# 32 tokens of a block leave the up products of a mixture-of-experts stage and are dotted on VectorE

## The chip, the cores and the metric

One core of one Trainium2 chip runs the kernel. The metric is the device time of one execution in microseconds (us). The kernel before took 1585.85, 1574.91 and 1577.71 us in three runs, median 1577.71 us.

## What is computed

A transformer block over 512 tokens of width 1024, all in float32: sliding-window attention and a gated delta rule side by side, an output projection, and then PEER, a layer that picks for each token 8 heads x 16 = 128 of 16384 experts. Only PEER is touched:

```
s_top, i_top = lax.top_k(s, 16)                      # per head and half of the query, of 128 keys
best_s, pos  = lax.top_k(sums of all 16 x 16 pairs, 16)
idx  = i1 * 128 + i2 ;  gate = softmax(best_s)
act  = gelu(einsum('tkd,td->tk', u_tab[idx], x))     # 128 dots of width 1024 for each token
out  = einsum('tk,tkd->td', act * gate, v_tab[idx])
```

## The kernel before

The 512 tokens lie in four blocks of 128. Block 0 is done by **gathering**: for each of its 128 pairs of a token, one indirect DMA on GpSimd's queue fetches a row of u and v for each of 128 tokens (8 KB a token, 1.05 MB), VectorE dots the u half with x and adds the v half, scaled, to a sum (`Gathered`, `dot` and `add`; `pair_steps` deals these 256 steps out by a table of rates). Six such rows are in SBUF.

Blocks 1 to 3 (`TD` = 384 tokens) are done **densely**: the table has 128 tiles of 128 experts, and for each tile TensorE multiplies all tokens by the tile's u ("up", 8 slices of the width x 3 products of high and low parts = 24 matmuls of 384 columns), ScalarE takes the gelu, VectorE multiplies by a gate that is zero where the expert was not chosen, and TensorE multiplies by the tile's v ("down", 18 matmuls of 512 columns into six banks). A float32 tile is split before it is multiplied: ScalarE rounds it to the high part, VectorE or GpSimd subtracts to get the low part.

The work runs in two stages behind the projections:

- **Routing** (`routing`). VectorE does the top-k selection, 13 parts for each block (`Selection.part`). For 48 batches of 8 tokens it writes two one-hot arrays (`one_hot`), ScalarE scales one by the gates (`gated`), and TensorE's **gate products** (16 matmul rows of 128 columns in the profile) make the dense gate matrix, which is stored to DRAM. To fill TensorE, the ups of the first `EARLY` = 80 tiles run here: 27 (`FIRST`) before the batches, one with each batch, 5 (`LAST`) after. Their gelus are stored to DRAM. The low parts of tiles 1 to 26 are made on GpSimd, all others on VectorE. A tile has 2 buffers for its parts and 4 (`NU`) for its raw rows; the up of tile t+2 can start only when up t is done, ScalarE has made its high part, and the low part is there.
- **Experts** (`experts`). 48 tiles with up and down, then 80 with the stored gelu and down alone. VectorE makes both low parts, the gate multiplication and the low part of the result, and runs block 0's steps beside (3.1 a tile in the first part, 1.0 in the second).

Orders are written out by hand, the same in each engine's program. Each DMA queue works in order: SP's has the loads and the gate stores, ScalarE's the gelu stores, GpSimd's the fetches. The one-hots compare with a row of 0..127 (`rt_iota_row`) in SBUF.

## Time and profile before

| | before |
|---|---|
| median of three runs | 1577.71 us |
| the profiled execution's span | 1581.1 us |
| PE, busy in matmuls | 1524.7 us, 96% |
| PEld, weight loads | 1388.1 us, 88% |
| DVE | 1326.5 us, 84% |
| ACT | 720.5 us, 46% |
| POOL | 339.2 us, 21% |
| bytes moved by DMA | 384.12 MB, 243 GB/s over the span |

PE is TensorE, DVE VectorE, ACT ScalarE, POOL GpSimd, SP the engine that only issues DMAs. A matmul's recorded duration overlaps its neighbours', so PE's cost is read from the distance between starts; the same holds to a smaller degree for DVE. Up to 409 us the kernel does the projections and the two mixers; nothing of that is touched. Routing runs from 409 to 851 us, the experts from there to 1577 us.

### The profile page before, as it was taken

What the parts mean: (1) busy time and instruction counts of PE and PEld (TensorE: products, weight loads), DVE (VectorE), ACT (ScalarE), POOL (GpSimd) and SP (SyncE); (2) the same over time, 40 slices, a digit from 0 to 9 for tenths busy, and PEclk for the clock granted to TensorE, in tenths of its full rate; (3) what the DMA queues carried; (4) which work ended last, traced back from release to release, by engine and by line L of the source; (5) the groups of instructions that cost most, each with busy time, mean ns of one, the idle gap of its engine ahead of it and who ended that gap; (6) DMA issues with size and microseconds to landing.
All of it is one profiled execution on the core that took longest, in us unless ns stands there. A gap on an engine that the chain in (4) does not pass through costs nothing. (4 is left out here: it accounts for less than half of the span.)

```text
span 1581.1 us, 24984 instructions
## 1 busy us (share of the span) xinstructions
PE 1524.7 (96%) x9451; PEld 1388.1 (88%) x9451; DVE 1326.5 (84%) x2360; ACT 720.5 (46%) x1442; POOL 339.2 (21%) x301
## 2 busy tenths in 40 slices
PE   7999799999999999999998999999999999999999
PEld 6898688889998999989998999999999888888887
DVE  4638777776799999988974999998989999999996
ACT  4553454141344698788763333333333334333332
POOL 4011620010466100301220222222322211111100
PEclk9999899999999999999999999999999999999999
DMA  5220004031444567878998999999998999999982
GB/s 197 86 81 1 8 29 160 30 111 50 132 165 153 168 196 214 316 241 282 366 366 312 334 360 354 341 352 328 372 339 315 354 407 376 380 363 340 351 290 97
DMA packets 152236, 384.12 MB, mean 243 GB/s; under 512 B 11072, under 2 KB 92096, under 8 KB 135488
## 3 DMA queue, kind: packets, MB, share of 16 engines
q1 hardware_dynamic: 122176, 232.75, 41.9%
q0 software_dynamic: 18432, 134.23, 23.4%
q10 hardware_dynamic: 11520, 15.73, 2.7%
q8 instruction: 65, 1.06, 0.3%
q14 instruction: 43, 0.35, 0.1%
HBM read 337.58 MB, written 45.09 MB: 242 GB/s over the span
## 5 line engine op out<-in xcount | busy, mean ns | idle before, releaser
L1795 POOL DMA_INDIRECT scores<-in_peer_uv,pair_index x86 | 126.2, 1468 | 620.2 <-DVE pair_sum L1819 503.2
L1984 PE MATMUL bank<-x_hi,u_split 128*128 128x384 f32 x640 | 220.3, 344 | 10.6 <-POOL u_split L1919 5.5
L1986 PE MATMUL bank<-x_hi,u_split 128*128 128x384 f32 x640 | 215.8, 337 | 0.0
L1985 PE MATMUL bank<-x_lo,u_split 128*128 128x384 f32 x640 | 215.6, 337 | 0.0
L2273 PE MATMUL bank<-v_hi,act_hi 128*128 128x512 f32 x528 | 206.2, 391 | 1.0 <-DVE v_lo L2336 1.0
L2275 PE MATMUL bank<-v_hi,act_lo 128*128 128x512 f32 x528 | 205.9, 390 | 0.0
L2274 PE MATMUL bank<-v_lo,act_hi 128*128 128x512 f32 x528 | 205.7, 390 | 0.0
L2352 DVE TENSOR_TENSOR act_tile<-gelu_tile,onehots 128x384 f32<-128x384 f32 x128 | 118.2, 923 | 43.8 <-ACT gelu_tile L2321 33.1
L2310 ACT ACTIVATE act_hi<-act_tile 128x384 fp32r<-128x384 f32 x128 | 66.6, 521 | 182.0 <-PE bank L2275 130.9
L1984 PEld LDWEIGHTS bank<-x_hi,u_split 128*128 128x128 f32 x640 | 121.0, 189 | 13.0 <-issue 5.9
L2261 PE MATMUL bank<-x_hi,u_split 128*128 128x384 f32 x384 | 129.1, 336 | 1.4 <-PEq L1929 1.4
L2263 PE MATMUL bank<-x_hi,u_split 128*128 128x384 f32 x384 | 129.0, 336 | 0.0
L2262 PE MATMUL bank<-x_lo,u_split 128*128 128x384 f32 x384 | 128.9, 336 | 0.0
L1985 PEld LDWEIGHTS bank<-x_lo,u_split 128*128 128x128 f32 x640 | 120.9, 189 | 0.0
L1986 PEld LDWEIGHTS bank<-x_hi,u_split 128*128 128x128 f32 x640 | 120.8, 189 | 0.0
L2050 ACT ACTIVATE onehot_gated<-onehot_i,rt_smallT 128x128 f32<-128x128 f32 x384 | 117.2, 395 | 6.3 <-DVE onehot_i L2102 4.2
L2275 PEld LDWEIGHTS bank<-v_hi,act_lo 128*128 128x128 f32 x528 | 99.1, 188 | 21.2
L2273 PEld LDWEIGHTS bank<-v_hi,act_hi 128*128 128x128 f32 x528 | 99.1, 188 | 20.7 <-issue 1.4
L2274 PEld LDWEIGHTS bank<-v_lo,act_hi 128*128 128x128 f32 x528 | 99.1, 188 | 19.4
L1819 DVE SCALAR_TENSOR_TENSOR pair_sum<-scores,pair_c,pair_sum 128x1024 f32<-128x1024 f32 x86 | 110.4, 1284 | 1.5
L2336 DVE TENSOR_TENSOR v_lo<-v_raw,v_hi 128x1024 fp32r<-128x1024 f32 x88 | 107.3, 1219 | 0.4 <-ACT v_hi L2304 0.4
L1802 DVE SCALAR_TENSOR_TENSOR scores<-scores,mix 128x1024 f32<-128x1024 f32 x86 | 104.8, 1219 | 0.0
(325 smaller groups left out, 3625.0 us busy)
## 6 DMA issues: line engine op xcount, KB each, us to landing
v_raw<-in_peer_v SPq DMA_DIRECT2D x128, 512.0 KB
u_raw<-in_peer_u SPq DMA_DIRECT2D x64, 512.0 KB, 7.0
u_raw_more<-in_peer_u SPq DMA_DIRECT2D x64, 512.0 KB, 6.7
gates<-gate_stage SPq DMA_DIRECT2D x24, 1024.0 KB, 6.0
onehots<-gates SPq DMA_DIRECT2D x32, 768.0 KB, 8.9
early_gelus<-early_gelu ACTq DMA_DIRECT2D x80, 192.0 KB
gelu_tile<-early_gelus SPq DMA_DIRECT2D x80, 192.0 KB
w_raw<-in_w_in SPq DMA_DIRECT2D x9, 1024.0 KB, 5.2
```

What stands on the lines that cost most here:

```text
L1795: pool.indirect_dma_start(self.slot(k), None, self.table, bass.IndirectOffsetOnAxis(ap=self.sidx[:, k:k + 1], axis=0)).then_inc(self.lande ...
L1984: nc.tensor.matmul(banks.bank(g)[:, 0:TD], uh[:, q, w], m.xh[:, k, P:], start=(k == 0), stop=False)
L1985: nc.tensor.matmul(banks.bank(g)[:, 0:TD], uh[:, q, w], m.xl[:, k, P:], start=False, stop=False)
L1986: t = nc.tensor.matmul(banks.bank(g)[:, 0:TD], ul[:, q, w], m.xh[:, k, P:], start=False, stop=(k == KD - 1))
L2050: ins = nc.scalar.activation(og[:, slot(b, k), t, :], oi[:, slot(b, k), t, :], ACT.Copy, scale=smallT[:, b % 2, 1, k * BT + t:k * BT + t + 1])
L2261: nc.tensor.matmul(bank, uh[:, q, w], m.xh[:, k, P:], start=(k == 0), stop=False)
L2262: nc.tensor.matmul(bank, uh[:, q, w], m.xl[:, k, P:], start=False, stop=False)
L2263: t = nc.tensor.matmul(bank, ul[:, q, w], m.xh[:, k, P:], start=False, stop=(k == KD - 1))
L2273: nc.tensor.matmul(bank[:], ah[:, s, w], v_hi[:, c], start=first, stop=False)
L2274: nc.tensor.matmul(bank[:], ah[:, s, w], v_lo[:, c], start=False, stop=False)
L2275: t = nc.tensor.matmul(bank[:], al[:, s, w], v_hi[:, c], start=False, stop=last)
L2352: nc.vector.tensor_tensor(af[:], ge[n % NG2][:], gt[:, it % 2, :, jj], ALU.mult).then_inc(gate_f, 1)
```

## The change

- 32 tokens (`NS`) of block 1 are no longer columns of the ups: each of the 128 tiles' 24 up matmuls has 352 columns (`TU`) in place of 384. The downs, the gate products and their one-hots stay as wide as they were.
- For these tokens their 32 x 128 chosen u rows are fetched: 32 indirect DMAs of 128 rows of 4 KB (`UpRows.fetch`), four sets of 32 pairs side by side in the 128 partitions. VectorE dots each with x (`UpRows.dot`), which a product with four unit matrices has laid four times over into two PSUM banks (`m.xs`). To have the indices of the four sets in place, six small DMAs are issued on GpSimd's queue (`move`). The activations times gates, transposed, take the place of the gates of these tokens in their four batches, which come last now, and so their column of the dense gate matrix is the finished activation.
- `EARLY` is 96: 21 ups before the batches, two with each batch whose number is below 32 and not 2 modulo 3, one with the others, 5 after. 54 more low parts in the batches are GpSimd's, tiles 1 to 20 as well: 74 in all.
- Selection goes through the blocks in the order 1, 2, 3, 0. Block 0's rows can be fetched only after that, behind all of GpSimd's low parts.
- The row 0..127, the row starts and the index steps, which VectorE reads together with a tile in SBUF, lie in PSUM bank 7; the routing stage has five banks for its products, not eight.
- The gelu stores go from ScalarE's queue to SP's, each behind the load of a later tile.
- In the experts' stage ScalarE copies each tile's gates into a contiguous tile (`copy_gate`), and VectorE multiplies in place there. There are 32 tiles with ups and 96 without; block 0's steps run at 3.1 and then at 1.5 a tile.

```diff
-EARLY = 80
+EARLY = 96
...
+NS = 32
+NR = P // NS
+TU = TD - NS
+CHOICE = [1, 2, 3, 0]
 GRP4 = 2
...
+    def place_constants(self, dve, bank):
+
+        link = self.link(dve)
+        self.iota, self.row0 = bank[:, 0:NK], bank[:, NK:NK + TOPK]
+        self.step = bank[:, 256:512].rearrange("p (q h a) -> p q h a", q=2, h=PH)
+        link(self.nc.vector.tensor_copy(self.iota, self.iota_made[:]))
+        link(self.nc.vector.tensor_copy(self.row0, self.row0_made[:]))
+
...
+
+        nc, link = self.nc, sel.link(dve)
+        link(nc.vector.scalar_tensor_tensor(sel.column[:], sel.small[:, 0, :], float(NK), sel.small[:, 2, :],
+                                            ALU.mult, ALU.add))
+        link(nc.vector.tensor_scalar(sel.column[:], sel.column[:], 2.0, None, ALU.mult))
+        nc.vector.tensor_copy(self.idx[0:NS, :], sel.column[0:NS, 0:NS])
+        nc.vector.tensor_copy(self.gate[0:NS, :], sel.small[0:NS, 1, 0:NS])
+        nc.vector.tensor_copy(sel.moved[0:NS, NS:], sel.column[0:NS, NS:]).then_inc(self.chosen, 1)
+
+    def move(self, pool, sel):
+
+        pool.wait_ge(self.chosen, 1)
+        for r in range(1, NR):
...
+            pool.dma_start(self.gate[rows, :], sel.small[0:NS, 1, cols]).then_inc(self.moved, 16)
+
+    def wait_moved(self, eng):
+        eng.wait_ge(self.moved, 2 * 16 * (NR - 1))
+
+    def fetch(self, pool, k):
+        n = len(self.slots)
+        if k >= n:
...
+            ap=self.idx[:, k:k + 1], axis=0)).then_inc(self.landed[k % n], 16)
+
+    def dot(self, dve, k):
+        n = len(self.slots)
+        dve.wait_ge(self.landed[k % n], 16 * (k // n + 1))
+        row = self.slots[k % n]
+        self.nc.vector.scalar_tensor_tensor(row, row, 1.0, self.xs, ALU.mult, ALU.mult,
...
-    in_first = todo[:sel.PARTS - AHEAD + sel.PARTS]
-    behind_1 = todo[len(in_first):][:4]
-    left = todo[len(in_first) + len(behind_1):]
+    LATE = 2 * NBT
+    ups_in = [1 if n >= LATE or n % 3 == 2 else 2 for n in range(NB_)]
+    FIRST = EARLY - sum(ups_in) - LAST
+    ups_of = [list(range(FIRST + sum(ups_in[:n]), FIRST + sum(ups_in[:n + 1]))) for n in range(NB_)]
+
+    pool_lows = list(range(1, FIRST)) + [t for n in range(LATE) for t in ups_of[n]]
...
+                def store_gelu(n):
+                    banks.wait_taken(sp, ("up", n))
+                    sp.dma_start(gelus[n], ge[:, n % 2, 0:TU]).then_inc(nxt.ge_out[n % 2], 16)
...
-                pool.wait_ge(sel.scores_read, 1)
+                def pool_low(t):
+                    pool.wait_ge(u_hi, t + 1)
+                    if t == 1:
+                        wait_low(pool, 0)
+                    u_low(nc.gpsimd, t).then_inc(low_by_pool, 1)
+
+                fetched = len(up_rows.slots)
+                for t in range(1, FIRST):
+                    pool_low(t)
+                    if t == TURN_1 + 2:
+                        up_rows.move(pool, sel)
+                    if t == TURN_1 + 3:
+                        up_rows.wait_moved(pool)
+                        for k in range(fetched):
+                            up_rows.fetch(pool, k)
+                for n in range(LATE):
+                    for t in ups_of[n]:
+                        pool_low(t)
+                    for k in range(fetched, min(NS, fetched + DOTS)):
+                        up_rows.fetch(pool, k)
+                        fetched += 1
+                pool.wait_ge(sel.chosen_0, 1)
+                pool.wait_ge(up_rows.dots, NS)
                 for k in range(nxt.fetched):
                     pairs_of_0.fetch(pool, k)
 
@@ -1977,14 +2101,13 @@
...
+                sel.place_constants(dve, ps[7])
...
-                pairs_out(1)
+                up_rows.choose(dve, sel)
+                for b, part in in_2:
+                    if part == 5:
+                        pairs_out(1)
+                    if part == 9:
+                        up_rows.wait_moved(dve)
+                    sel.part(dve, b, part)
+                    if part >= sel.PARTS - DOTS_FIRST:
+                        up_rows.dot(dve, part - sel.PARTS + DOTS_FIRST)
                 first_keys(0)
-                for b, part in behind_1:
-                    sel.part(dve, b, part)
-                dve.wait_ge(u_lo, FIRST)
-                early_low(FIRST)
                 for n in range(NB_):
                     if n + 1 < NB_:
                         first_keys(n + 1)
-                    wait_products(dve, n)
+                    wait_products(dve, n - RING)
                     one_hot(oj, n, 2).then_inc(oj_ready, 1)
-                    early_low(early(n) + 1)
+                    for t in range(ups_of[n][-1] + 1, EARLY - LAST if n + 1 == NB_ else ups_of[n + 1][-1] + 1):
+                        if not low_count[t][0]:
+                            early_low(t)
+                    if n + 1 == NB_:
+                        early_low(EARLY - LAST)
                     if n in beside:
                         sel.part(dve, *beside[n])
                     for c in small_after(n - 1):
                         pairs_out(c)
-                    if n >= 2 * NBT:
-                        pairs_of_0.vector_steps(dve, steps[n - 2 * NBT])
+                    for k in dots_in[n]:
+                        up_rows.dot(dve, k)
+                    if n == COEFS - 1:
+                        up_rows.coefficients(dve)
+                    if n == COEFS + 1:
+                        coefs_out()
+                    if n >= LATE:
+                        pairs_of_0.vector_steps(dve, steps[n - LATE])
                 for n in range(EARLY - LAST + 1, EARLY + 1):
                     early_low(n)
 
...
+                def copy_gate(n):
+                    it, jj = n // BODY, n % BODY
+                    if jj == 0:
+                        act.wait_ge(g_in[it % 2], 32 * (it // 2 + 1))
+                    if n >= 2:
+                        act.wait_ge(gated, n - 1)
+                    else:
+                        act.wait_ge(nxt.ge_out[n], 16 * (EARLY // 2))
+                    nc.scalar.activation(af[n % 2][:], gt[:, it % 2, :, jj], ACT.Copy).then_inc(gate_cols, 1)
...
+                    dve.wait_ge(gate_cols, n + 1)
+                    nc.vector.tensor_tensor(af[n % 2][:, NS:], ge[n % NG2][:], af[n % 2][:, NS:], ALU.mult).then_inc(gate_f, 1)
...
-        rates = [2.0] * (P // 8) + [1.0, 2.0] + [3.1] * (NK - EARLY - 2) + [1.0] * EARLY
+        rates = [2.0] * (P // 8) + [1.0, 2.0] + [3.1] * (NK - EARLY - 2) + [1.5] * EARLY
```

The order of instructions shows this at three places. First GpSimd's program at the start of routing, `u_split` being the low parts. Before:

```order
L1919 TENSOR_TENSOR u_split<-u_raw,u_split 128x1024 x2
L1919 TENSOR_TENSOR u_split<-u_raw_more,u_split 128x1024 x2
L1919 TENSOR_TENSOR u_split<-u_raw,u_split 128x1024 x2
L1919 TENSOR_TENSOR u_split<-u_raw_more,u_split 128x1024
L1795 DMA scores<-in_peer_uv,pair_index 128x2048 x4
L1795 DMA pair_rows<-in_peer_uv,pair_index 128x2048 x2
L1795 DMA scores<-in_peer_uv,pair_index 128x2048 x4
```

After:

```order
L2008 TENSOR_TENSOR u_split<-u_raw,u_split 128x1024
L1868 DMA up_index<-shared_index_moved 32x32
L1869 DMA up_gate<-rt_small 32x32
L1868 DMA up_index<-shared_index_moved 32x32
L1869 DMA up_gate<-rt_small 32x32
L1868 DMA up_index<-shared_index_moved 32x32
L1869 DMA up_gate<-rt_small 32x32
L2008 TENSOR_TENSOR u_split<-u_raw,u_split 128x1024
L1878 DMA pair_rows<-in_peer_uv,up_index 128x1024 x4
L2008 TENSOR_TENSOR u_split<-u_raw_more,u_split 128x1024 x2
```

Six small DMAs and then four fetches now stand between low parts that TensorE waits for. The second place is VectorE's program for two early batches, beside which parts of the selection run. Before:

```order
L1392 MAX top<-scores 128x8 x16
L2102 TENSOR_TENSOR onehot_i<-rt_iota_row,rt_smallT 128x1024
L2102 TENSOR_TENSOR onehot_j<-rt_iota_row,rt_smallT 128x1024
L1919 TENSOR_TENSOR u_split<-u_raw,u_split 128x1024
L1397 MAX_INDEX top_index<-top,scores 128x8 x16
L2102 TENSOR_TENSOR onehot_i<-rt_iota_row,rt_smallT 128x1024
L2102 TENSOR_TENSOR onehot_j<-rt_iota_row,rt_smallT 128x1024
L1919 TENSOR_TENSOR u_split<-u_raw_more,u_split 128x1024
```

After:

```order
L2244 TENSOR_TENSOR onehot_i<-bank,rt_smallT 128x1024
L2244 TENSOR_TENSOR onehot_j<-bank,rt_smallT 128x1024
L1401 MAX top<-scores 128x8 x16
L1885 SCALAR_TENSOR_TENSOR pair_rows,up_s<-pair_rows,banks 128x1024 x2
L2244 TENSOR_TENSOR onehot_i<-bank,rt_smallT 128x1024
L2244 TENSOR_TENSOR onehot_j<-bank,rt_smallT 128x1024
L1406 MAX_INDEX top_index<-top,scores 128x8 x16
L1885 SCALAR_TENSOR_TENSOR pair_rows,up_s<-pair_rows,banks 128x1024 x2
```

The low part is gone, two dots with fetched rows (`pair_rows`) stand in its place, and the one-hots read a bank. The third place is SP's DMA queue between two gate stores. Before:

```order
L1937 DMA u_raw<-in_peer_u 128x1024
L1937 DMA u_raw_more<-in_peer_u 128x1024
L1949 DMA gates<-gate_stage 128x16x128
L1937 DMA u_raw_more<-in_peer_u 128x1024
L1937 DMA u_raw<-in_peer_u 128x1024
L1949 DMA gates<-gate_stage 128x16x128
```

After:

```order
L2042 DMA gates<-gate_stage 128x16x128
L2029 DMA u_raw_more<-in_peer_u 128x1024
L2035 DMA early_gelus<-early_gelu 128x352
L2029 DMA u_raw<-in_peer_u 128x1024
L2035 DMA early_gelus<-early_gelu 128x352
L2029 DMA u_raw<-in_peer_u 128x1024
L2035 DMA early_gelus<-early_gelu 128x352
L2042 DMA gates<-gate_stage 128x16x128
L2029 DMA u_raw_more<-in_peer_u 128x1024
```

A gelu store stands behind every load of a tile now, in the same queue.

## Rows read from the trace of the kernel before

**Rows 1.** Windows; busy us of PE, PEld, DVE, ACT, POOL; clock, DMA share, GB/s.
```profile
532.00:824.00 292.00, 285.61 (x1911) 282.95 (x1911) 273.65 (x569) 235.91 (x586) 37.89 (x20) 1.00 0.81 271
...
851.00:1235.00 384.00, 384.00 (x1963) 351.70 (x1963) 346.71 (x435) 137.91 (x223) 104.53 (x71) 1.00 0.93 339
1235.00:1577.00 342.00, 340.96 (x1492) 279.67 (x1491) 314.05 (x393) 124.25 (x184) 40.19 (x36) 1.00 0.89 330
```
**Rows 2.** Timeline of PE (start, duration in us, engine, line), experts' stage.
```profile
1003.77 0.39 PE L2273 MATMUL bank<-v_hi,act_hi 128*128 128x512 f32 x1
...
1007.86 0.34 PE L2261 MATMUL bank<-x_hi,u_split 128*128 128x384 f32 x1
...
1012.02 0.39 PE L2273 MATMUL bank<-v_hi,act_hi 128*128 128x512 f32 x1
```
**Rows 3.** Timeline of PE in the query product, 256 columns wide.
```profile
384.74 0.28 PE L1551 MATMUL bank<-x_hi,w_oq_h 128*128 128x256 f32 x1
...
388.46 0.28 PE L1552 MATMUL bank<-x_lo,w_oq_h 128*128 128x256 f32 x1
```
**Rows 4.** Timeline of PE, routing; in brackets the idle time before and its releaser.
```profile
408.98 0.45 PE L1984 MATMUL bank<-x_hi,u_split 128*128 128x384 f32 x1 [0.19 <-DVE u_split L1919]
...
532.86 1.95 PE L2011 MATMUL bank<-onehot_j,onehot_gated 128*128 128x128 f32 x16
...
815.87 1.95 PE L2011 MATMUL bank<-onehot_j,onehot_gated 128*128 128x128 f32 x16
...
821.81 1.95 PE L2011 MATMUL bank<-onehot_j,onehot_gated 128*128 128x128 f32 x16
...
835.13 0.41 PE L1984 MATMUL bank<-x_hi,u_split 128*128 128x384 f32 x1 [3.05 <-DVE u_split L1919]
```
**Rows 5.** DVE groups by form (busy us, mean ns), of 409:508 and of 530:715.
```profile
L1443 DVE TENSOR_TENSOR selectors<-selectors,index_steps 128x256 f32<-128x256 f32 x32 | 28.4, 957 | 0.1
...
L1443 DVE TENSOR_TENSOR selectors<-selectors,index_steps 128x256 f32<-128x256 f32 x32 | 11.1, 421 | 0.0
```
**Rows 6.** Timeline of POOL: low parts, then fetches of rows.
```profile
437.19 4.08 POOL L1919 TENSOR_TENSOR u_split<-u_raw_more,u_split 128x1024 fp32r<-128x1024 f32 x1 [1.72 <-ACT u_split L2030]
...
455.32 2.44 POOL L1919 TENSOR_TENSOR u_split<-u_raw_more,u_split 128x1024 fp32r<-128x1024 f32 x1 [1.72 <-ACT u_split L2030]
...
640.27 8.49 POOL L1795 DMA_INDIRECT scores<-in_peer_uv,pair_index  x1 [116.03 <-DVE top_index L1397]
649.06 0.94 POOL L1795 DMA_INDIRECT scores<-in_peer_uv,pair_index  x1 [0.30 <-issue]
...
736.79 1.68 POOL L1795 DMA_INDIRECT scores<-in_peer_uv,pair_index  x1 [80.60 <-DVE pair_sum L1819]
```
**Rows 7.** Windows within those stages, same columns.
```profile
1250.00:1310.00 60.00, 60.00 (x264) 49.22 (x263) 57.18 (x73) 23.53 (x35) 8.10 (x8) 1.00 1.02 401
1310.00:1400.00 90.00, 90.00 (x395) 73.91 (x394) 86.71 (x111) 34.76 (x52) 11.24 (x11) 1.00 0.99 373
1400.00:1500.00 100.00, 100.00 (x439) 82.06 (x438) 93.04 (x116) 36.19 (x55) 14.45 (x12) 1.00 0.97 349
743.00:827.00 84.00, 83.27 (x559) 82.79 (x558) 75.39 (x85) 63.26 (x158) 23.04 (x14) 1.00 1.04 367
```
**Rows 8.** DMA issues, 415:505 and 790:850; last number: median us to landing.
```profile
u_raw_more<-in_peer_u SPq DMA_DIRECT2D x10, 512.0 KB, 3.5
...
u_raw<-in_peer_u SPq DMA_DIRECT2D x5, 512.0 KB, 14.7
```
**Rows 9.** DVE groups by form of 1400:1500, then of 0:409.
```profile
L2352 DVE TENSOR_TENSOR act_tile<-gelu_tile,onehots 128x384 f32<-128x384 f32 x24 | 22.2, 923 | 2.6
...
L2356 DVE TENSOR_TENSOR act_lo<-act_tile,act_hi 128x384 fp32r<-128x384 f32 x24 | 13.4, 559 | 4.2 <-ACT act_hi L2310 4.2
L1819 DVE SCALAR_TENSOR_TENSOR pair_sum<-scores,pair_c,pair_sum 128x1024 f32<-128x1024 f32 x8 | 10.3, 1284 | 0.1
...
L1701 DVE TENSOR_TENSOR acc<-acc,bank 128x512 f32<-128x512 f32 x8 | 5.5, 686 | 5.6 <-PE bank L1553 5.6
```

More of the change, by code:

```diff
@@ L340, in _ @@
                 pool.wait_ge(pads, 1)
-                link = chain(pool, plink, [0])
+                link = chain(pool, *m.own["pool"])
                 for b in range(TB):
@@ L362, in _ @@
             def _(act):
-                link = chain(act, alink, [0])
+                link = chain(act, *m.own["act"])
                 def split_w(n):
@@ L470, in _ @@
             def _(dve):
-                link = chain(dve, vlink, [0])
+                link = chain(dve, *m.own["dve"])
                 def split_w(n):
@@ L955, in _ @@
                         level(l, b)
-                link = chain(pool, plink, [0])
+                link = chain(pool, *m.own["pool"])
                 for b in range(TB):
@@ L964, in _ @@
             def _(dve):
-                link = chain(dve, vlink, [0])
+                link = chain(dve, *m.own["dve"])
                 def att_max(b):
@@ L1186, in _ @@
             def _(dve):
-                link = chain(dve, vlink, [0])
+                link = chain(dve, *m.own["dve"])
                 def z_gain(b):
@@ L1266, in _ @@
             def _(pool):
-                link = chain(pool, plink, [0])
+                link = chain(pool, *m.own["pool"])
                 for b in range(TB):
@@ L1682, in _ @@
                 sel.constants(pool)
-                link = chain(pool, plink, [0])
+                for r in range(NR):
+                    nc.gpsimd.tensor_copy(m.repeat[0:NS, r * NS:(r + 1) * NS], m.ident[0:NS, 0:NS])
+                link = chain(pool, *m.own["pool"])
                 for b in range(TB):
@@ L2084, in _ @@
                             sel.exps(act, b)
-                evict(NB_ - 1)
-                pairs_of_0.scalar_steps(act, steps[NBT - 1])
+                    if n == LAST_DOT + 1:
+                        up_rows.gelu(act)
                 for n in range(EARLY - LAST, EARLY):
@@ L2392, in hybrid_layer @@
         m.mem = mem
+        m.own = {name: (sem(f"{name}_in_order"), [0]) for name in ("dve", "pool", "act")}
         m.ident = mem.take("ident", [P, P])
         m.neg_half = mem.take("neg_half", [P, 1])
+        m.repeat = mem.take("unit_rows", [P, P])
         m.upper = mem.take("upper", [P, P])
```

371 lines of the change are left out of this document (217 added, 154 removed).

## The prediction

> **What bounds the kernel.** I read the windows by stage first. In the experts' stage TensorE is busy in every microsecond (384.00 of 384) and in the routing stage nearly so (285.61 of 292), with VectorE close behind (346.71 and 273.65) [rows 1]. Then the timeline of PE, for the distance between starts. In the experts' stage 18 downs of 512 columns take 4.09 us, 227 ns each, and 24 ups of 384 columns take 4.16 us, 173.3 ns each [rows 2]. The query product of 256 columns starts 31 matmuls in 3.72 us, 120.0 ns each [rows 3]. That is 13.3 ns and 0.417 ns a column over the whole range, so a narrower up is cheaper in full proportion. Last I read where TensorE waits in routing: the first gate products start at 532.86, 123.9 us after the first up, and 28 ups of 4.16 make 116.5 of it, so 7.4 are waits; one undisturbed batch takes 5.94 us, 47 batches last 288.95 us, so 9.8 are waits; one late load costs 3.05 us near the end [rows 4].
>
> **The ups.** 128 tiles x 24 matmuls x 32 columns x 0.417 ns = **-41.0 us**; an up then takes 3.84 us. The number of ups does not change, only 16 of them move ahead of the experts' stage, at the same price. The gate products stay at 5.94 - 4.16 = 1.78 us a batch.
>
> **The start of routing.** 22 ups lie before the first gate product now, 84.5 us. Each up needs its predecessor but one, a high part on ScalarE and a low part on GpSimd (2.44 us [rows 6]). About 1.4 us of GpSimd's time a tile is free (3.84 - 2.44). Between low parts 12 and 13 stand the six small DMAs. The first fetch of the old kernel took 8.49 us, one right behind it 0.94, with 0.30 between them [rows 6], so I take 8.49 + 5 x 1.24 + 0.30 = 15.0 us; less the free 1.4 that is 13.6 late for low part 13, and up 13, gelu 13 and every later split queue behind it. The four fetches behind low part 13 are 5.0, 3.6 late. With 0.1 a tile for the tighter chain (2 us) and 2 us for a clock that may fall in a pause of 13 us, TensorE waits 21 us there, against 7.4: **+14 us**. VectorE's part of this stage hides under it: it has four parts of selection fewer, four dots more, and its products of selectors with index steps ran at 957 ns beside GpSimd's low parts and at 421 ns without them [rows 5]. Bounds: if nothing is paid for the first DMA and VectorE is then what is waited for, +2; if the indirect form pays its own 7.5, +21.
> The Trainium skill (GPSIMD Engine Reference, Instruction dispatch) says that the first call of freshly loaded GpSimd code pays about 6 us more. The row's 8.49 against 0.94 agrees in kind; with the page's 6 the sum would be 1.5 us lower.
>
> **The batches.** VectorE loses the low part of each of the first 32 batches and gets two dots in 14 of them. GpSimd does two low parts and two fetches in a batch with two ups: 4.9 + 2 x 1.24 to 2 x 1.68 [rows 6] = 7.4 to 8.2 us of the batch's 2 x 3.84 + 1.78 = 9.46. A fetch stands behind the second low part of its batch, and the dot in VectorE's same batch waits for its landing; the unloaded landing of a 0.5 MB load is 3.5 us, with full queues 14.7 [rows 8]. Behind the dots VectorE has the next one-hots, for which the gate products wait. From one batch's second up over high part, low part, fetches, landing, dots and one-hots I count about 13 us and the landing, for two batches of 16.2 us in the mean: a landing of 4 us is hidden, 6 us is not. The one-hot reads its constant from a bank; VectorE's sum with a bank takes 686 ns for 512 columns [rows 9], no more a column than two tiles in SBUF, so 0. I take 7 us of waits for the 9.8 of before, **-3 us**; the ends are -6 and, with landings of 7 us in 14 batches, +15.
>
> **The end of routing.** From 743 to 827 the queues moved 367 GB/s at a DMA share of 1.04, with TensorE just fed [rows 7]. The old kernel fetched block 0's first six rows at 640, in slack. The new one can do so only behind the last low part of batch 31. From there to the last up I count 8.4 MB of u, 2.9 of gelus, 8.4 of gates, 2.1 of v, 20 rows of 1.05 MB and 4.3 for the five last ups: 47 MB, of which 4 may land later. 43 MB at 367 GB/s are 117 us; TensorE's work there is 16 x 5.62 + 5 x 3.84 = 109. A part of the wait was there before (3.05 us [rows 4]): **+7 us**, between 0 and 15. Gelu stores sit behind loads in SP's queue now; where these land after 14.7 us [rows 8], the gelu of two tiles later waits for its buffer, which is in the upper end.
>
> **The last tiles.** In the 96 tiles without ups a tile takes TensorE 4.09 us. It needs 0.524 MB of v, 0.197 of gates, 0.180 of gelu and 0.75 rows of 1.049: 1.69 MB, 412 GB/s, for the 85 tiles in which 128 steps of block 0 are left. Before it was 1.44 MB. The most that was moved while TensorE stayed full was 401 GB/s over 60 us [rows 7]: 85 x 1.69 / 401 = 358 us, not 348. **+10 us**; 0 if more can be moved, +37 at the 373 GB/s of the next window [rows 7]. VectorE is a second bound at the same place: 93.04 us in 100 [rows 7] or 3.81 a tile, less 0.41 for the gate multiplication (923 ns from a strided tile, a contiguous one 559 [rows 9]), plus half a step of 1.28 [rows 9]: 4.04 of 4.09.
> The Trainium skill (SBUF — State Buffer, A bandwidth-pool intuition) gives about 358 GB/s from HBM to one core; the tail would cost 52 us more by it. The trace moved 401, so the measurement decides.
>
> **Sum.** -41 + 14 - 3 + 7 + 10 = -13 us against the profiled span of 1581.1, which lies 3.4 over the median. From the median 1577.7 that is 1564.7; I forecast 1564 us, 0.9% faster.
>
> **Rivals.**
> - *Small insertions and transfers are hidden.* The six DMAs cost little, or more than 401 GB/s can be moved. -41 + 2 to 6 - 3 + 3 + 3 gives about 1542 to 1548. For it: TensorE did not wait once in the 60 us at 401 GB/s. Against it: 8.49 us is in the rows.
> - *The last tiles are bound by transfers.* At 373 GB/s the sum is 27 higher, 1591. For it: that window followed the one at 401, and the share was 0.99; against it, less was asked for there.
> - *GpSimd becomes the bound* (slower). A low part took 4.08 us where VectorE's products with two operands in SBUF ran beside it [rows 6, 5]. At 4.1 us a batch with two ups needs 8.2 + 3.0 = 11.2 us of GpSimd for 9.46, 1.7 too much in ten batches and 17 us; at the start the chain is 0.8 a tile longer, 16 us. That gives 1564 + 33 = 1597. It decides from a mean of 3.2 us on. Against it: these operands lie in a bank now, and with them VectorE reads SBUF once. The Trainium skill (SBUF — State Buffer, Who interferes with whom) says the same: only a VectorE instruction with two inputs in SBUF, or in a two-port mode, blocks GpSimd's reads. By that rule low parts stay near 2.44; the trace agrees with its first half.
> - *The change does not do what it says:* if a narrow up keeps its 173.3 ns, because the weights' load sets the pace, all else costs 28 us and it is 1605. Against it: 120.0 ns at 256 columns [rows 3].
>
> **Chances.** The forecast's case 0.5, from 1552 to 1576; hidden 0.2; tail bound by transfers 0.13; GpSimd 0.13; no cheaper up 0.04. About 1% is what a measurement of this kernel can tell from no change: below 1562 is faster, above 1593.5 slower. Faster: 0.2 and not quite half of 0.5, 0.43. Slower: 0.15. Same: 0.42. The range from 1538 to 1592 leaves out GpSimd's case and the last one, and the low edge of the hidden one.
>
> **What would show it.** Up starts 160 ns apart; a pause of some 13 us of TensorE near 455 us with GpSimd in its six DMAs; the first gate product near 512; low parts of 2.4 to 2.6 us; products with index steps near 421 ns throughout; VectorE's dots in the first 14 batches waiting for a row by 1 to 3 us or not at all; loads landing after 12 us and more from 800 us on; tiles of 4.2 us in the last stage at about 400 GB/s, with VectorE over 95% busy. The forecast is wrong if low parts pass 3.2 us, if the tail's tiles are 4.09 us or over 4.4, or if TensorE's pause at the six DMAs isn't there.

## The result and the profile after

The changed kernel took 1586.06 us, the median of seven runs (1583.91 to 1589.55), against 1580.68 us for the kernel before in seven runs beside it. The ratio is 1.004 with a 95% interval of 1.0021 to 1.0059. It is a little slower, where 0.9% faster was forecast. The profiled spans are 1582.4 us after and 1581.1 before.

The page of the changed kernel, its part on engines:

```profile
PE 1502.0 (95%) x9438; PEld 1354.3 (86%) x9438; DVE 1242.8 (79%) x2392; ACT 826.7 (52%) x1571; POOL 462.7 (29%) x391
```

TensorE has 22.7 us less of recorded work than before and is not done sooner. VectorE has 84 us less. So the totals do not say where the time went. The same stretches as in [rows 1], cut where the changed kernel changes its pace (columns as there):

```profile
408.00:502.00 94.00, 89.08 (x535) 86.49 (x535) 91.86 (x380) 39.77 (x58) 60.77 (x33) 0.98 0.60 192
502.00:650.00 148.00, 132.77 (x862) 129.94 (x861) 121.87 (x348) 91.86 (x213) 88.15 (x54) 0.97 0.84 274
650.00:790.00 140.00, 140.00 (x958) 140.00 (x958) 85.28 (x245) 97.64 (x228) 71.81 (x33) 1.00 0.71 217
790.00:890.00 100.00, 91.51 (x624) 89.64 (x623) 88.28 (x100) 71.31 (x185) 13.51 (x15) 0.97 1.05 390
1185.00:1225.00 40.00, 34.24 (x141) 27.45 (x140) 31.77 (x46) 19.78 (x28) 7.41 (x6) 0.91 1.01 409
1225.00:1500.00 275.00, 275.00 (x1196) 223.80 (x1195) 262.82 (x383) 162.38 (x227) 61.93 (x50) 1.00 1.02 413
```

TensorE runs short most in the second, the fourth and the fifth row, and the granted clock falls a little there. In the third and the last it is full, in the last at 413 GB/s. The timeline of PE has the places themselves, the answers to [rows 2] and [rows 4]:

```profile
461.17 0.40 PE L2108 MATMUL bank<-x_hi,u_split 128*128 128x352 f32 x1 [1.45 <-POOL u_split L2008]
468.58 0.40 PE L2108 MATMUL bank<-x_hi,u_split 128*128 128x352 f32 x1 [3.33 <-POOL u_split L2008]
...
501.67 1.05 PE L2127 MATMUL bank<-onehot_j,onehot_gated 128*128 128x128 f32 x8
...
815.76 2.05 PE L2127 MATMUL bank<-onehot_j,onehot_gated 128*128 128x128 f32 x8 [6.46 <-ACT onehot_gated L2183]
...
914.00 0.40 PE L2420 MATMUL bank<-x_hi,u_split 128*128 128x352 f32 x1 [2.26 <-PEq L2021]
...
1003.92 0.33 PE L2420 MATMUL bank<-x_hi,u_split 128*128 128x352 f32 x1
...
1007.76 0.39 PE L2432 MATMUL bank<-v_hi,act_hi 128*128 128x512 f32 x1
...
1011.89 0.33 PE L2420 MATMUL bank<-x_hi,u_split 128*128 128x352 f32 x1
...
1212.12 0.77 PE L2432 MATMUL bank<-v_hi_late,act_hi 128*128 128x512 f32 x1 [5.76 <-DVE v_lo_late L2508]
```

24 ups take 3.84 us (1003.92 to 1007.76), as forecast, and a tile with up and down 7.97 us (1003.92 to 1011.89) for the old 8.25. So I add up TensorE's waits: the length of a stretch, less 3.84 us for each up (4.16 before) and 1.78 for each batch's gate products. For the experts it is 7.93 or 4.09 a tile (8.25 before). A fall of the clock is in the wait.

| TensorE's waits, us | before | after | difference | forecast |
|---|---|---|---|---|
| first up to first gate product | 7.4 | 9.1 | +1.7 | +14 |
| batches up to 780 us | 8.5 | 23.7 | +15.2 | -3 |
| last batches and last five ups | 7.7 | 19.1 | +11.4 | +7 |
| experts | 3.7 | 18.6 | +14.9 | +10 |
| sum | 27.3 | 70.5 | +43.2 | +28 |

Against 43.2 us of new waits stand 41.0 us of narrower ups. The first up also started 0.85 us earlier (408.13 against 408.98). That makes +1.3, and so do the spans. The medians lie 5.4 us apart.

### The profile page after: what moved, and what is told of

It reads as the page before. It is cut to its first block, busy times and chain, and to the rows that moved or that the text cites. A ratio compares the mean times of both kernels' runs of the same rounds, so it can differ in the third digit from the quotient of the medians.

```text
span 1582.4 us, 25236 instructions
## 1 busy us (share of the span) xinstructions
PE 1502.0 (95%) x9438; PEld 1354.3 (86%) x9438; DVE 1242.8 (79%) x2392; ACT 826.7 (52%) x1571; POOL 462.7 (29%) x391
## 4 chain that ended last, share of the span: by engine, by line
PE 59%; DVE 6%; DMA 3%; issue 2%; POOL 1%; SPq 1%; ACT 1%; ACTq 0%; DVEq 0%; POOLq 0%
PE bank L2433 7%; PE bank L2434 7%; PE bank L2432 7%; PE bank L2108 6%; PE bank L2109 6%; PE bank L2110 6%; PE bank L2127 4%; PE banks L2432 3%; PE banks L2433 3%; PE banks L2434 3%; PE bank L2420 2%; PE bank L2422 2%; PE bank L2421 2%; DMA v_raw<-in_peer_v 1%; DVE pair_sum L1828 1%
## 5 line engine op out<-in xcount | busy, mean ns | idle before, releaser
L2108 PE MATMUL bank<-x_hi,u_split 128*128 128x352 f32 x768 | 258.3, 336 | 7.1 <-POOL u_split L2008 4.8
L2109 PE MATMUL bank<-x_lo,u_split 128*128 128x352 f32 x768 | 250.5, 326 | 0.0
L2110 PE MATMUL bank<-x_hi,u_split 128*128 128x352 f32 x768 | 250.0, 326 | 0.0
L2479 ACT ACTIVATE act_tile<-onehots 128x384 f32<-128x384 f32 x128 | 122.3, 955 | 62.3 <-DVE act_lo L2521 58.0
L2008 POOL TENSOR_TENSOR u_split<-u_raw,u_split 128x1024 fp32r<-128x1024 f32 x37 | 89.9, 2430 | 135.3 <-ACT u_split L2165 77.0
L2432 PE MATMUL bank<-v_hi,act_hi 128*128 128x512 f32 x320 | 124.8, 390 | 1.2 <-DVE v_lo L2508 1.2
L2127 PE MATMUL bank<-onehot_j,onehot_gated 128*128 128x128 f32 x768 | 102.8, 283 | 23.7 <-issue 15.2
L2434 PE MATMUL bank<-v_hi,act_lo 128*128 128x512 f32 x320 | 125.3, 392 | 0.0
L2127 PEld LDWEIGHTS bank<-onehot_j,onehot_gated 128*128 128x128 f32 x768 | 97.0, 197 | 28.4 <-issue 28.0
L2008 POOL TENSOR_TENSOR u_split<-u_raw_more,u_split 128x1024 fp32r<-128x1024 f32 x37 | 89.8, 2428 | 73.2 <-ACT u_split L2165 73.1
L2463 ACT ACTIVATE v_hi<-v_raw 128x1024 fp32r<-128x1024 f32 x80 | 84.2, 1053 | 14.4 <-DMA v_raw<-in_peer_v 14.1
## 6 DMA issues: line engine op xcount, KB each, us to landing
v_raw<-in_peer_v SPq DMA_DIRECT2D x128, 512.0 KB, 10.6
```

Source lines behind the costliest of these rows:

```text
L2008: return on.tensor_tensor(ul[:, n % 2, :], u_raw[n % NU], uh[:, n % 2, :].bitcast(F32), ALU.subtract)
L2108: nc.tensor.matmul(out, uh[:, q, w], m.xh[:, k, P + NS:], start=(k == 0), stop=False)
L2109: nc.tensor.matmul(out, uh[:, q, w], m.xl[:, k, P + NS:], start=False, stop=False)
L2110: t = nc.tensor.matmul(out, ul[:, q, w], m.xh[:, k, P + NS:], start=False, stop=(k == KD - 1))
L2127: t = nc.tensor.matmul(banks.bank(g)[:, q * NK:(q + 1) * NK], og[:, n % RING, 4 * i + q, :], oj[:, n % RING, 4 * i + q, :], start=True, st ...
L2432: nc.tensor.matmul(bank[:], ah[:, s, w], v_hi[:, c], start=first, stop=False)
```

## Who waits for whom

Between 501 and 650 us, the waits of the changed kernel (in all, times, longest):

```profile
DVE pair_rows L1885 <- DMA pair_rows<-in_peer_uv,up_index: 25.4, 12, 6.6
ACT onehot_gated L2183 <- DVE onehot_i L2244: 25.1, 12, 4.7
PE bank L2127 <- issue: 15.2, 10, 3.2
```

VectorE waits for a fetched row. ScalarE then waits for VectorE's one-hots. For TensorE's waits the profile names no releaser ("issue"), but its gate products need the one-hots of both. The row of `UpRows.fetch` (all 32 of its fetches) says why, and beside it stands what a load of u took in that stretch:

```profile
DMA to landing us min/median/max: 5.3/6.7/9.1
...
u_raw<-in_peer_u SPq DMA_DIRECT2D x12, 512.0 KB, 4.2
```

A fetch of 0.52 MB by 128 indices landed after 6.7 us in the median (6.9 for the 28 of this stretch), a plain load of as much after 4.2. At the hand-over to block 0, from 790 to 890 us:

```profile
ACT early_gelu L2175 <- DMA early_gelus<-early_gelu: 25.4, 9, 7.6
...
PE bank L2127 <- ACT onehot_gated L2183: 8.3, 4, 6.5
```

ScalarE stands before a gelu whose buffer a store has not left. In the experts' stage, SP's queue, ScalarE and the v loads near the hole at 1212:

```profile
1185.23 0.53 SPq L2392 DMA_DIRECT2D h_rows<-h_spill  x1
...
1188.04 0.33 SPq L2358 DMA_DIRECT2D v_raw<-in_peer_v  x1
...
1209.66 1.06 ACT L2463 ACTIVATE v_hi_late<-v_raw 128x1024 fp32r<-128x1024 f32 x1 [7.48 <-DMA v_raw<-in_peer_v]
```

From 1154 to 1227 us the v loads landed after 8.9 us in the median and after 21.6 at the longest. The longest is the load issued at 1188.04: it lands at 1209.64, where ScalarE goes on. 2.8 us ahead of it stands the residual h, 2.1 MB. The kernel before reads h at the same place of its program (four tiles into its last stage):

```profile
1259.90 0.50 SPq L2233 DMA_DIRECT2D h_rows<-h_spill  x1
```

It paid nothing there: TensorE was full from 1250 to 1310 us [rows 7].

## Experiments

All twelve are edits of the changed kernel. Ratios are against the kernel before, run on the same chip. The changed kernel itself stands at 1.004 (1586.06 us), with an interval of 1.0021 to 1.0059. The runs came in four sets, in which the kernel before took 1576.6 to 1579.6 us in the median. So a time of one set against a time of another is good to some 2 us.

**The dots one batch later.**

```
-        dots_in[(k - DOTS_FIRST) // DOTS].append(k)
-    LAST_DOT = (NS - 1 - DOTS_FIRST) // DOTS
+        dots_in[(k - DOTS_FIRST) // DOTS + 1].append(k)
+    LAST_DOT = (NS - 1 - DOTS_FIRST) // DOTS + 1
```

> The changed kernel with one edit: in the batches each pair of dots with fetched rows is one batch later on VectorE (batches 1 to 14), so that a row has a batch longer to land; the fetches stay. In the changed kernel's trace VectorE stood 25.4 us before 12 of its dots for rows that landed 6.7 us after their issue, and TensorE had 22 us of waits between 501.7 and 648 us. Theory A (landing of the rows): both go, the time is 15 to 22 us lower, near 1567. Theory B (GpSimd's queue of two low parts and two fetches, 7.4 to 8.2 us a batch, is what holds the batches): the dots' waits go, but the gate products wait as before for one-hots behind low and high parts, and the time is within 5 us of the changed kernel's, 1581 to 1587.

1566.54 us, ratio 0.9906 [0.987, 0.9943]. This one edit makes the changed kernel faster than the one before. Waits from 501 to 650 us:

```profile
DVE pair_rows L1885 <- DMA pair_rows<-in_peer_uv,up_index: 6.5, 6, 2.0
```

TensorE's waits between the first gate product and 660 us fell from 23.6 to 6.2 us, though the rows landed no sooner (7.0 us in the median for 6.9). At the hand-over to block 0 they grew by some 4 us. Theory A holds: the landing was what the loop could not hide. Theory B falls, because GpSimd's queue was as full as before.

**The gelu stores on ScalarE's queue.**

```
-                    store_gelu(n)
...
+                    banks.wait_taken(act, ("up", n))
+                    act.dma_start(gelus[n], ge[:, n % 2, 0:TU]).then_inc(nxt.ge_out[n % 2], 16)
```

> The changed kernel with one edit: the gelu stores go from ScalarE's own queue again, as in the kernel before. In the changed kernel's trace ScalarE stood 41.3 us in 17 places before a gelu whose buffer a store in SP's queue still held (7.6 us at 805, where TensorE then waited 6.5), none in the kernel before. Theory A (the store's place behind loads and gate stores in one queue): those waits fall to under 5 us, the hand-over at 795 to 831 us loses its 11 us of TensorE's waits and the last ups 2 to 4 of their 6; the time is 10 to 16 us lower, 1570 to 1576. Theory B (the DMA engines themselves are full there, share 1.04 to 1.06, whichever queue asks): the waits move to loads, tiles or rows, and the time is at most 3 us lower.

1583.18 us, ratio 1.0018 [0.9994, 1.0043]. That is 3 us under the changed kernel, with intervals that overlap. The last ups did lose 4.6 of their 6.1 us of waits. The hand-over kept its 12.8, with another wait in the gelu's place:

```profile
817.10 0.60 ACT L2192 ACTIVATE gate_stage<-bank 128x512 f32<-128x512 f32 x1 [10.24 <-DMA gates<-gate_stage]
```

So Theory B at the hand-over: whichever store is next there comes late. The queue alone was not its cause.

**h read back ten tiles before the end.**

```
-                    if n == NMT + 4:
+                    if n == NK - 10:
```

> The changed kernel with one edit: the residual h (2.1 MB) is read back ten tiles before the end, not four tiles into the last stage, where no rows of block 0 are fetched any more. In the changed kernel's trace one v tile landed 21.6 us after its issue at 1200 us, 15 us behind that transfer, and TensorE stood 5.8 us and then ran at 1.2 GHz for a while: a tile of 10.00 and one of 6.34 us for two of 4.15. Theory A (the 2.1 MB in front of the v loads in a stage that moves 412 GB/s anyway): the hole goes, 7 to 8 us less, 1578 to 1579. Theory B (the last stage asks for more than can be moved until its buffers have run dry once): the hole comes at another place, and the time stays within 2 us of 1586.

The expectation puts the late v load's issue at 1200 us; it was 1188.04. 1579.47 us, ratio 1.000 [0.9983, 1.0017], 6 us less. The window of the hole:

```profile
1185.00:1225.00 40.00, 40.00 (x176) 32.66 (x175) 39.23 (x57) 23.45 (x33) 9.14 (x8) 1.00 1.02 416
```

PE is busy 40.00 of 40 where it was 34.24, and no hole came elsewhere in that stage, whose waits fell from 18.6 to 10.6 us. Theory A.

**All ups 384 columns wide again** (the gelu still takes 352 of them).

```
-    q, out = n % 2, banks.bank(g)[:, 0:TU]
+    q, out = n % 2, banks.bank(g)[:, 0:TD]
```

> The changed kernel with one edit: all ups multiply 384 columns again, and the gelu takes the 352 of them that it took; all else, the fetched rows too, is as changed. It prices the narrowing alone. Prediction's term (0.417 ns a column): the time is 36 to 41 us higher, 1622 to 1627; starts of ups 173 ns apart. Rival (TensorE's waits for rows, stores and low parts are in part filled by wider ups, so that the narrowing is worth less in this kernel than its columns): 20 to 33 us higher, 1606 to 1619, with fewer waits between 501 and 650 us.

1612.47 us, ratio 1.0192 [1.0152, 1.0232]. That is 26 us more (24 by the ratios), not 41: the rival. The 96 ups up to the experts' stage cost 30.7 us more, but TensorE's waits there fell from 51.9 to 40.3. So a third of what the narrow ups save was time in which wide ones would have covered a wait. In the experts' stage the price came to 7.9 us.

**Block 0's first six rows, one a batch from batch 26 on.**

```
+    ROWS_AT = [(26 + k, k) for k in range(6)]
...
+                    for at, k in ROWS_AT:
+                        if at == n:
+                            pairs_of_0.fetch(pool, k)
```

> The changed kernel with one edit: block 0's first six rows (1.05 MB each) are fetched one behind each of GpSimd's low parts of batches 26 to 31, not all behind the last. In the changed kernel they were issued from 779.4 to 786.4 us, and from 785 on the queues moved 386 and 397 GB/s at a share of 0.99 and 1.05; gelu stores, loads of u and gate stores then landed late, and TensorE had 11 us of waits from 795 to 831. Moving the gelu stores alone did not help: the gate store behind which ScalarE waited took 17.9 us then. Theory A (the burst of six rows fills the DMA engines just where 2.1 MB of v are read too): with the rows landing before 780, TensorE's waits there fall to 0 to 3 us, the time to 1575 to 1578. Theory B (the steady demand behind batch 32, a row and a half a batch, u, v, stores, is what the engines can't keep up with): the same wait comes a few batches later, and the time stays within 3 us of 1586.

1581.94 us, ratio 1.0012 [0.999, 1.0035], 4 us less with intervals that overlap, between the two theories. First the window of the hand-over in the changed kernel, then in this one:

```profile
785.00:820.00 35.00, 27.33 (x178) 26.79 (x177) 23.66 (x29) 18.42 (x46) 5.69 (x5) 0.91 1.03 402
```

```profile
785.00:820.00 35.00, 33.64 (x239) 33.48 (x238) 32.56 (x36) 24.57 (x63) 3.75 (x4) 1.00 0.99 347
```

Without the burst TensorE is nearly full there. Of the 13.0 us of waits behind 780 us 7.7 were left, now from 817 to 832 us, and 2.4 had moved ahead of 780.

**The four v tiles spread over batches 37 to 46.**

```
-                        for i in range(len(m.v_raw)):
+                    if n in (LATE + 5, LATE + 8, LATE + 11, LATE + 14):
```

> The changed kernel with one edit: the first four v tiles of the experts' stage (0.52 MB each) are read at batches 37, 40, 43 and 46, not all four at batch 32. Theory A (these four loads, in front of the gelu store in SP's queue, are what TensorE waits for by 6.5 us at 815.8): the hand-over loses 5 to 8 of its 11 us of waits, the time is 1578 to 1581. Theory B (the rows' burst is the cause, the four loads 2 of some 14 MB in those 35 us): at most 3 us less at the hand-over, and some of it comes back as later loads of u in front of the last ups: 1583 to 1588.

1588.19 us, ratio 1.0067 [1.0047, 1.0087]. Theory B: no gain, and if anything a loss of 2 to 4 us (the intervals overlap). The wait at the hand-over stayed (6.9 us until 817.60), and new ones of 1.9 and 2.5 us came at 852 and 877.

**The row 0..127 in SBUF again.**

```
-        self.iota, self.row0 = bank[:, 0:NK], bank[:, NK:NK + TOPK]
+        self.iota, self.row0 = self.iota_made[:], bank[:, NK:NK + TOPK]
```

> The changed kernel with one edit: the row 0..127 that the one-hots (two of 1.22 us a batch) and the selection compare with is read from SBUF again, not from bank 7, so that these products have two operands in SBUF. It tests the rival on GpSimd and the 8.49 us of a fetch in the kernel before. Theory A (VectorE with two SBUF operands holds up GpSimd): a low part that runs beside a pair of one-hots takes 2 us longer, near 4.7 against 2.43; with two low parts, two fetches and two pairs of one-hots in GpSimd's time of a batch, GpSimd needs 9.5 to 12 us for 9.46 in the batches with two ups and becomes what TensorE waits for: the time is 10 to 40 us higher, 1596 to 1626, and some fetches take 2 to 4 us in place of 0.95. Theory B (no such hold-up, the long low parts and the 8.49 us had another cause, such as the first use of a DMA): low parts and fetches stay at 2.43 and 0.95, the time within 3 us of 1586.

1603.63 us, ratio 1.015 [1.0123, 1.0176], 17 us more. GpSimd's low parts (duration in ns, min/median/max), first of the changed kernel and then of this one:

```profile
L2008 POOL TENSOR_TENSOR u_split<-u_raw_more,u_split x37: 2373/2430/2451, 413.5 to 776.9; 128x1024 fp32r<-128x1024 f32 x37
```

```profile
L2007 POOL TENSOR_TENSOR u_split<-u_raw_more,u_split x37: 2357/2435/4434, 415.8 to 795.7; 128x1024 fp32r<-128x1024 f32 x37
```

The median is the same, but 22 of all 74 low parts take over 2.5 us, up to 4.43. VectorE pays too. Its one-hots of the i half, in the changed kernel and in this one:

```profile
L2244 DVE TENSOR_TENSOR onehot_i<-bank,rt_smallT x44: 1214/1219/1225, 495.7 to 855.4; 128x1024 f32<-128x1024 f32 x44
```

```profile
L2243 DVE TENSOR_TENSOR onehot_i<-rt_iota_row,rt_smallT x44: 1208/1221/3496, 502.1 to 874.8; 128x1024 f32<-128x1024 f32 x44
```

Of all 96 one-hots 17 took 1.55 to 3.50 us. In the changed kernel none took over 1.24, and none in the kernel before either, whose GpSimd makes no low parts in the batches. Theory A in kind, with 17 us near its lower end. The row 0..127 in a bank, which I had priced at nothing either way, earns 17 us in this kernel. What the row starts and the index steps earn there is not shown by a run, but VectorE's products with the index steps took 957 ns beside GpSimd's low parts before [rows 5] and take 414 now:

```profile
L1449 DVE TENSOR_TENSOR selectors<-selectors,bank 128x256 f32<-128x256 f32 x32 | 10.9, 414 | 0.1
```

**Five edits together**: the dots later, h late, the six rows and the v tiles as above, and at the start one fetch behind each of low parts 13 to 16.

```
-                        for k in range(fetched):
-                            up_rows.fetch(pool, k)
...
+                    if TURN_1 + 3 <= t < TURN_1 + 3 + fetched:
+                        up_rows.fetch(pool, t - TURN_1 - 3)
```

> The changed kernel with five edits: the dots a batch later, h read back ten tiles before the end, block 0's first six rows one a batch from batch 26 on, the four v tiles spread over batches 37 to 46, and at the start one fetch behind each of low parts 13 to 16 in place of four behind 13. If the causes are separate places of TensorE's wait, they add up: 20 us for the dots (measured), 5 for h (measured), 8 to 11 for the hand-over, 2 to 4 for the start: 1545 to 1552, 2% faster than the kernel before. If what is gained ahead of the hand-over is lost to it (the same bytes in less time before batch 32), it is 1558 to 1568.

1555.87 us, ratio 0.9853 [0.983, 0.9877]. It is 30 us under the changed kernel: the gains for the most part add up, yet the start gave none. The first gate product of this kernel:

```profile
501.26 2.05 PE L2133 MATMUL bank<-onehot_j,onehot_gated 128*128 128x128 f32 x8 [4.50 <-DVE onehot_j L2250]
```

The wait of 3.33 us for low part 14 (468.58) is gone, and TensorE waits 4.50 for VectorE's first one-hots instead.

**The five edits with wide ups.**

> The kernel with the five edits (e8) and all ups 384 columns wide again, as in e4. It prices the narrowing where most of TensorE's waits are gone. Between the changed kernel and e4 the narrowing was worth 26 us, not 41. Theory A (the missing part was time in which wider ups would have covered waits: 5 us in the batches, 5 at their end and in the last ups): here it is worth more, 33 to 40 us over e8's 1555.9, so 1589 to 1596. Theory B (the narrowing is worth less than its columns whatever waits there are, since a switch between kinds of matmul costs the same): again 24 to 30 us, 1580 to 1586.

1575.44 us, ratio 0.9987 [0.9977, 0.9998]: 20 us over the last one. Neither theory holds. I had expected the narrowing to be worth more with fewer waits around it, and it is worth less. Its first gate product:

```profile
501.53 1.05 PE L2133 MATMUL bank<-onehot_j,onehot_gated 128*128 128x128 f32 x8
```

22 ups wider by 0.32 us each, 7 us in all, and the gate product is 0.27 us later. TensorE's waits there are 2.1 us against 8.8. In the rest of routing they are 10.9 against 21.2. So 17 of the 30.7 us come back, and the experts' stage costs 8.3 us. VectorE sets the end of the start, and in the batches other loops still set part of the pace. I had thought of the waits as something outside TensorE's own speed. They are also what a faster TensorE is left with.

**The five edits and the gelu stores on ScalarE's queue.**

> The kernel with the five edits (e8) and the gelu stores on ScalarE's queue, as in e2. In e8 ScalarE still waits 22.9 us in nine places from 820 to 895 us for a gelu store behind loads in SP's queue, and TensorE 5.6 at the end of the batches and 5.0 in the last ups. Theory A (with the burst gone the store's place in the queue matters): 4 to 8 us less than 1555.9, 1548 to 1552. Theory B (as in e2, the wait moves to a gate store or a load): within 2 us of 1555.9.

1544.69 us, ratio 0.9796 [0.9777, 0.9814]. That is 11 us less (9 by the ratios), beyond Theory A. The same edit brought 3 us before the burst and the dots were moved. The waits fell from 8.2 to 3.4 us up to 660, from 3.4 to 0.1 up to 780, from 4.7 to 2.7 in the last batches and from 5.0 to 1.5 in the last ups. So more of the gain lies in the batches (8.1 us) than behind them (5.5), and the experts' stage gave 1 us back. ScalarE's waits for a gelu's buffer fell from 43.8 us in 20 places to 1.8 in three.

**The first four dots behind the first one-hots.**

```
-                    if part >= sel.PARTS - DOTS_FIRST:
-                        up_rows.dot(dve, part - sel.PARTS + DOTS_FIRST)
...
+    dots_in[0] = list(range(DOTS_FIRST))
```

> The kernel with the five edits (e8) and the first four dots, that stand between the last parts of VectorE's first two blocks of selection, behind the one-hots of the first batch. In e8 spreading the first four fetches took away TensorE's wait of 3.3 us at 468 us, but TensorE then waited 4.5 us at 501.3 for the first one-hots, and the first gate product came no earlier than in the changed kernel: 22 ups with 8.8 us of waits against 9.1. Theory A (VectorE is the bound of the start): the first gate product comes 4 to 5 us earlier, the total 3 to 5 us lower, 1551 to 1553. Theory B (the dots are only moved to where VectorE is as full): the wait comes back at the next one-hots, within 2 us of 1555.9.

1555.59 us, ratio 0.9856 [0.9826, 0.9885], as without it. The first gate product came 4.5 us earlier from the first up on, and 3.6 and 1.6 us of new waits follow at 502 and 507. That is Theory B's time, but not its cause. TensorE waited for a low part of GpSimd, and GpSimd stood before a fetch:

```profile
502.21 0.95 POOL L1878 DMA_INDIRECT pair_rows<-in_peer_uv,up_index  x1 [4.85 <-DVE pair_rows L1885]
```

The fetched rows have four buffers. The fifth fetch can start only when the first dot is done, which now came at 502, and the next low part stands behind that fetch. Whether the moved dots pay with these fetches moved too was not tried.

**Both.**

> The kernel with the five edits (e8), the gelu stores on ScalarE's queue (e10, 1544.7) and the first four dots behind the first one-hots (e11). e11 brought the first gate product 4.5 us forward and then lost the same in the next batches, where VectorE and the gelu stores in SP's queue held it; e10 has 5 us fewer waits in those batches. Theory A (that slack is enough for the four dots): 3 to 4 us below e10, 1541 to 1542. Theory B (VectorE is full up to the end of the fetched rows' dots, and a dot moved by one batch only moves the wait): within 1.5 us of 1544.7.

1541.54 us, ratio 0.9744 [0.9704, 0.9784]. It is the fastest kernel of the study, 2.6% under the one before. GpSimd's wait is there again (4.86 us before the fetch at 501.78). Whether this kernel beats the 1544.69 is open: the intervals overlap and the profiled spans are 1540.6 and 1541.2 us. The gelu stores' queue is shown to be worth having, the moved dots are not.

## Why the prediction was wrong

The middle of the forecast was 22 us too low. Some 15 of them are in the terms: the start came 12 lower than forecast, the batches 18 higher, the end of routing 4 and the experts' stage 5. The other 7 are the distance of the two profiled executions from their medians (1581.1 against 1577.7 before, 1582.4 against 1586.06 after). The mechanisms were nearly all named, and the terms were mis-sized, the largest in the batches. That the start's error offset two thirds of theirs is luck.

- **The ups, -41.** 160 ns between starts and 3.84 us an up: right. In tiles with up and down it was 0.28 us and not 0.32, since 7.97 is not 7.93. What failed is to take the term as if TensorE were the bound in every stretch. Put back to 384 columns, the ups cost 24 to 26 us in this kernel and 20 in the improved one.
- **Start of routing, +14, came as +1.7.** The step that failed is "so I take 8.49 + 5 x 1.24 + 0.30 = 15.0 us". On GpSimd:

```profile
455.34 0.80 POOL L1868 DMA_DIRECT2D up_index<-shared_index_moved  x1
456.14 0.53 POOL L1869 DMA_DIRECT2D up_gate<-rt_small  x1
...
461.21 1.08 POOL L1878 DMA_INDIRECT pair_rows<-in_peer_uv,up_index  x1 [0.18 <-issue]
```

  The six took 3.3 us, and the first indirect fetch 1.08. TensorE's pause near 461 is 1.45 us and not 13. The prediction had named the absence of this pause as a sign that the forecast is wrong. The four fetches cost 3.33 us, near the 3.6 foreseen. The 8.49 us of [rows 6] was no price of a first DMA. In the kernel before VectorE did this beside it:

```profile
639.87 1.22 DVE L2102 TENSOR_TENSOR onehot_i<-rt_iota_row,rt_smallT 128x1024 f32<-128x1024 f32 x1
...
646.67 1.00 DVE L1405 TENSOR_TENSOR sums<-top 128x128 f32<-128x128 f32 x7
647.71 0.99 DVE L1409 MAX8 best<-sums 128x8 f32<-128x50 f32 x8
```

  From 639.87 to 647.67 VectorE had 13 products in a row that read both operands from SBUF. The fetch that was begun at 640.27 ended at 648.76, one fetch's 0.94 us and a little behind the last of them. With the row 0..127 in SBUF again, fetches of 1.65 and 1.97 us for 0.94 came beside such products (800.80, 802.76). The changed kernel has the same within one burst, with the row in a bank:

```profile
781.94 1.66 POOL L1804 DMA_INDIRECT scores<-in_peer_uv,pair_index  x1 [0.31 <-issue]
783.90 0.94 POOL L1804 DMA_INDIRECT scores<-in_peer_uv,pair_index  x1 [0.30 <-issue]
```

  Beside the first VectorE made a low part, both operands in SBUF (781.56, 1.23 us), beside the second a one-hot that reads the bank (783.84, 1.22 us). The edit of the row shows it too: 5 of the 32 fetches of u rows took 1.76 to 1.94 us with the row in SBUF, and none over 1.08 with it in the bank. So VectorE's products with both operands in SBUF hold up GpSimd's indirect DMAs. That 13 in a row make 8.49 us is inferred from the times above and was not tried by itself. The size of the lower end, "nothing is paid for the first DMA and VectorE is then what is waited for, +2", is what came, with another wait: TensorE still waited for GpSimd (1.45 and 3.33 us). VectorE stood close behind, as the 4.50 us in the run with five edits show. The Trainium skill (GPSIMD Engine Reference, Instruction dispatch), whose 6 us for the first call of freshly loaded code I had weighed there, is not borne out for these DMAs: the first direct one took 0.80 us and the first indirect one 1.08.
- **Batches, -3, came as +15.2.** The loop was in the prediction: "a landing of 4 us is hidden, 6 us is not". The step that failed is the landing put into it. I took it near the 3.5 us of a plain load [rows 8] and so "7 us of waits". Rows fetched by index landed after 6.7 us in the median. The +15 was written down as the upper end, and the run with the dots a batch later gives it back.
- **End of routing, +7, came as +11.4.** The sum written down gives 117 - 109 - 3 = +5, not +7. The step that failed is that bytes over rate give the mean of a stretch, but the stretch has a burst of 6.3 MB at its head. The last five ups had their 6.1 us before the change as well (6.5). What was new is the hand-over, and at least two waits stand behind it: the six rows (4 us alone), and the gelu stores in SP's queue once the rest is out of the way (some 5 of the 11 us that the move then earned; the other 8 of waits were in the batches, where the prediction had no term for these stores).
- **Last tiles, +10, came as +14.9 for the whole stage, by another mechanism.** "The most that was moved while TensorE stayed full was 401 GB/s" was no ceiling. 413 GB/s were moved over 275 us with TensorE full. The tiles' own demand cost next to nothing. The reload of h in front of the v loads cost 8.0 us (tiles of 10.00 and 6.34 for two of 4.15) and was in no term of the prediction: it had cost nothing before. The rest of the 18.6 is 2.4 before the first down, 1.5 in four tiles at the stage's change, 1.3 in the tiles with ups, 5.3 in 4.145 us for 4.09 a tile. In the 80 tiles before it was 4.118 us a tile, 2.2 in all. What makes it longer is open: it goes on to the end, where the queues move 98 and then 42 GB/s and VectorE is busy half of the time or less. VectorE was nearer to being the bound than written: 923 less 559 ns is 0.36 us and not 0.41, which gives 4.09 of 4.09 us for the forecast's 4.04. It was busy in 262.82 of 275 us.
- **The rivals.** GpSimd as the bound did not come, low parts stayed at 2.43 us, and its price with the condition put back was 17 us where I had 33. The Trainium skill (SBUF — State Buffer, Who interferes with whom) had the rule, and the run with the row in SBUF agrees with it (low parts of up to 4.43 us for 2.43). The hidden case was half right (start and tail) and fell on the landing, the burst and h. The tail bound by transfers did not come either.

## What to carry to other kernels

When a loop is closed through a DMA, price the landing by a transfer of the same kind: one fetched by 128 indices took 6.7 us where a plain one of as many bytes took 4.2. If it is not certain, put a whole step between issue and use, which was worth 20 us here. Making the bound engine faster earns its full term only where it is bound; sum its work over each stretch apart and ask what ends the stretch otherwise. A one-time load that was free in a stage with slack has to be priced again when the stage moves more: h cost 8.0 us in a stage that moves 413 GB/s. And buffers couple engines: a dot moved behind the one-hots held the next fetch, and the fetch held a low part.

## What had not been expected of the hardware

The core moved 413 GB/s for 275 us with TensorE full, above the 401 that [rows 7] showed and the 358 of the Trainium skill (SBUF — State Buffer, A bandwidth-pool intuition). VectorE products with both operands in SBUF cost GpSimd and VectorE both: low parts up to 4.43 us for 2.43, fetches 1.9 for 0.94, one-hots up to 3.50 for 1.22. Moving one operand to PSUM was worth 17 us in 1600. The granted clock was 0.97 over the 148 us of the first batches and 0.91 over the 35 of the hand-over, where TensorE had waits of 1 to 6 us, and 1.00 wherever it was full. A wait there can cost more than its own length: behind the 5.76 us at 1212.12 the downs started 0.43 us apart, 0.23 from 1217 on, with a granted clock of 0.67 from 1212 to 1219.
